# K's inverse norms as rows through DRAM from the third head on, and all of these transfers on SyncE's queue

## The reference, cut to what matters

```python
kv = _rmsnorm(x, kv_norm) @ w_kv
k_sh = _rmsnorm(kv[..., :QK_WIDTH].reshape(b, s, N_HEADS, 2, HEAD_DIM), k_norm)
...
q = (h @ w_q).reshape(b, s, N_HEADS, 2, HEAD_DIM)
q = _rmsnorm(q, q_norm) * (HEAD_DIM ** -0.5)
sc = jnp.einsum('bqhcd,bkhcd->bhcqk', qi, k).astype(jnp.float32)
...
p = jax.nn.softmax(sc, axis=-1)
a = p[:, :, 0] - lam * p[:, :, 1]
...
o = _rmsnorm(o, subln) * (1.0 - lambda_init)
```

## Time and profile before

| what | value |
| --- | --- |
| time, median of 3 runs (lowest, highest) | 941.27 us (940.96, 941.45) |
| the profiled execution, its own time | 941.54 us |
| its span in the profile | 939.7 us |
| PE busy, share of the span | 934.1 us, 99% |
| PEld (weight loads) | 771.6 us, 82% |
| DVE | 683.8 us, 73% |
| ACT | 470.7 us, 50% |
| POOL | 89.8 us, 10% |
| chain that ended last: PE, DVE, ACT, DMA, issue | 91%, 4%, 2%, 2%, 1% |
| DMA queue of SyncE (q1) | 85632 packets, 98.31 MB |
| DMA queue of ScalarE (q10) | 1824 packets, 1.61 MB |

### The profile page before, as it was taken

How to read it: one execution, slowest core, us unless ns; L and a number is a source line. 1 busy time by engine, 2 the same in 40 slices (tenths; PEclk the granted TensorE clock), 3 DMA queues, 4 the chain that set the end, 5 groups by cost and what they waited for, 6 DMA issues and landing times.

```text
span 939.7 us, 11721 instructions
## 1 busy us (share of the span) xinstructions
PE 934.1 (99%) x4439; PEld 771.6 (82%) x4439; DVE 683.8 (73%) x989; ACT 470.7 (50%) x614; POOL 89.8 (10%) x70
## 2 busy tenths in 40 slices
PE   9999999999999999999999999999999999999998
PEld 7888888888888888888888887888888888888887
DVE  6876766676676689988887886757766676667685
ACT  7644343333434438787777773535334333433441
POOL 3000000100000002123222220000100000010010
PEclk9999999999999999999999999999999999999999
DMA  7328682494556644233333232336485458248535
GB/s 258 105 90 239 153 234 90 99 264 129 135 142 173 179 85 120 71 107 93 102 103 103 90 101 90 90 91 188 126 248 155 122 121 250 90 92 225 175 90 135
DMA packets 101583, 130.45 MB, mean 139 GB/s; under 512 B 4297, under 2 KB 63481, under 8 KB 101537
## 3 DMA queue, kind: packets, MB, share of 16 engines
q1 hardware_dynamic: 85632, 98.31, 32.0%
q0 software_dynamic: 14080, 29.91, 17.5%
q10 hardware_dynamic: 1824, 1.61, 0.7%
HBM read 127.69 MB, written 4.75 MB: 141 GB/s over the span
## 4 chain that ended last, share of the span: by engine, by line
PE 91%; DVE 4%; ACT 2%; DMA 2%; issue 1%; SPq 0%; ACTq 0%; DVEq 0%
PE bank L1695 28%; PE bank L1697 28%; PE bank L1696 28%; PE bank L1967 2%; PE bank L1957 1%; DMA raw<-in_w_mlp_out_dram 1%; DVE w_low L1080 1%; PE bank L1996 1%; DMA work<-in_x_dram 1%; PE bank L1872 1%; DVE a_low_buf L1163 0%; ACT w_high L729 0%; ACT w_high L666 0%; PE bank L1938 0%; PE bank L1806 0%
## 5 line engine op out<-in xcount | busy, mean ns | idle before, releaser
L1695 PE MATMUL bank<-h_high_buf,w_high 128*128 128x512 f32 x640 | 252.2, 394 | 0.0
L1697 PE MATMUL bank<-h_high_buf,w_low 128*128 128x512 f32 x640 | 249.5, 390 | 0.0
L1696 PE MATMUL bank<-h_low_buf,w_high 128*128 128x512 f32 x640 | 249.1, 389 | 0.0
L1695 PE MATMUL bank<-w_high,a_high_buf 128*128 128x512 f32 (+1 forms) x452 | 176.1, 390 | 0.1
L1697 PE MATMUL bank<-w_high,a_low_buf 128*128 128x512 f32 (+1 forms) x452 | 175.1, 387 | 0.0
L1696 PE MATMUL bank<-w_low,a_high_buf 128*128 128x512 f32 (+1 forms) x452 | 175.1, 387 | 0.0
L1080 DVE TENSOR_TENSOR w_low<-raw,w_high 128x2048 fp32r<-128x2048 f32 (+2 forms) x56 | 120.3, 2148 | 51.4 <-ACT w_high L729 31.8
L1695 PEld LDWEIGHTS bank<-h_high_buf,w_high 128*128 128x128 f32 x640 | 120.2, 188 | 26.5 <-issue 2.2
L1697 PEld LDWEIGHTS bank<-h_high_buf,w_low 128*128 128x128 f32 x640 | 120.1, 188 | 25.5
L1696 PEld LDWEIGHTS bank<-h_low_buf,w_high 128*128 128x128 f32 x640 | 120.3, 188 | 24.1
L738 ACT ACTIVATE work<-work 128x512 f32<-128x512 f32 x64 | 40.0, 632 | 177.9 <-DVE work L1147 177.9
(11 more groups left out here) (187 smaller groups left out, 1162.5 us busy)
## 6 DMA issues: line engine op xcount, KB each, us to landing
raw<-in_w_mlp_out_dram SPq DMA_DIRECT2D x24, 1024.0 KB, 6.8
raw<-in_w_mlp_out_dram POOLq DMA_DIRECT2D x24, 1024.0 KB, 8.5
raw<-in_w_mlp_in_dram SPq DMA_DIRECT2D x16, 1024.0 KB, 6.2
work<-in_w_mlp_out_dram SPq DMA_DIRECT2D x8, 1024.0 KB, 5.1
work<-in_w_mlp_in_dram SPq DMA_DIRECT2D x8, 1024.0 KB, 7.6
raw<-in_w_kv_dram SPq DMA_DIRECT2D x16, 512.0 KB, 4.0
xT<-in_w_mlp_out_dram SPq DMA_DIRECT2D x8, 1024.0 KB, 4.8
xT<-in_w_mlp_in_dram SPq DMA_DIRECT2D x8, 1024.0 KB, 7.0
```

The source lines that it names most:

```text
L1695: pe.matmul(acc, w_hi, m_hi, start=start, stop=False, skip_group_check=onto)
L1696: pe.matmul(acc, w_hi, m_lo, start=False, stop=False, skip_group_check=onto)
L1697: return pe.matmul(acc, w_lo, m_hi, start=False, stop=stop, skip_group_check=onto)
```

## The change

From the third head on (n = 2 to 7, made in passes 1 to 6), K's inverse norms take the way through DRAM that o's take:

- K's part and Q's part of the statistics are separate: `k_sums`, `k_roots`, `k_inverses`, then `q_sums`, `q_roots`, `q_inverses`. K's come first on VectorE and ScalarE.
- The turn of K's squares moves from behind Q's projection into it, between its fifth and sixth step. The turn back of the spread inverses and the spreading copy are gone.
- The reciprocal writes K's 8 columns grouped by vector; SyncE stores them as two rows of 512 in DRAM (128x2x4 numbers) and loads each row into 64 partitions of `ksq`. VectorE multiplies `kf` by `ksq` read with a step of four (`k_norm_rows`).
- Both transfers of o's row move from ScalarE's queue to SyncE's. The order on SyncE in a pass is: K and Q's weights, K's rows, V's weights, o's row.
- GpSimd's subtraction of K's half of the weights also waits for `k_inverse` of the same pass.

```diff
 # SyncE
+            def spread_k_rows(n):
+
+                sp.wait_ge(k_inverse, n - 1)
+                sp.dma_start(k_row.rearrange("c (p i) -> p c i", p=P), kq_rstd_buf[:, 0:8].rearrange("p (c i) -> p c i", c=2))\
+                  .then_inc(k_row_stored, 16)
+                sp.wait_ge(k_row_stored, 16 * n - 16)
+                sp.wait_ge(kn_ready, n)
+                for c in range(2):
+                    sp.dma_start(ksq[c * HD:(c + 1) * HD, :], k_row[c:c + 1, :].to_broadcast([HD, S])).then_inc(k_row_landed, 16)
...
+            with sp.Fori(4, H) as n:
+                load_kq(n)
+                spread_k_rows(n - 1)
+                load_v(n)
+                spread_o_row(n - 3)
 # GpSimd
+                if h >= 2:
+                    pool.wait_ge(k_inverse, h - 1)
 # ScalarE, head
                     split_high_first(n + 1, kq_landed(n + 1))
+                k_roots(n)
                 square_q(n)
...
-                kq_roots(n)
+                q_roots(n)
...
-                store_o_row(h - 1)
...
-                load_o_row(h - 1)
 # VectorE
+            def k_inverses(n):
+
+                dve.wait_ge(k_rooted, n - 1)
+                dve.reciprocal(kq_rstd_buf[:, 0:8].rearrange("p (c i) -> p i c", c=2), kq_root_buf[:, 0:8].rearrange("p (i c) -> p i c", c=2))\
+                   .then_inc(k_inverse, 1)
...
+            def k_norm_rows(n):
+
+                dve.wait_ge(k_row_landed, 32 * n - 32)
+                k = kf.rearrange("p (i n) -> p i n", i=TT)
+                dve.tensor_tensor(k, k, ksq.rearrange("p (n i) -> p i n", i=TT), ALU.mult).then_inc(kn_ready, 1)
...
                     split_low(U_HEAD + 1 + 2 * n, 0, 1024)
+                    k_sums(n, I[0])
                     o_sums(h - 1, I[3])
-                kq_sums(n, I[0], O[3], first)
-                kq_inverses(n)
+                    k_inverses(n)
+                    q_low(n)
+                    q_sums(n, O[3])
+                    q_inverses(n)
...
-                k_norm(n, I[0])
+                if first:
+                    k_norm(n, I[0])
+                else:
+                    k_norm_rows(n)
 # TensorE
+                    project(None, 1, 1024, I[1], a_high_buf, a_low_buf, None, range(0, 5))
+                    turn_ksq(n, I[0])
+                    project(None, 1, 1024, I[1], a_high_buf, a_low_buf, w_used, range(5, KC))
...
-                turn(ksq, I[0], k_spread, n, k_turned)
```

More of the change, by code:

```diff
@@ L240, in build_program @@
         SUM_BANK = [I[0], I[1], I[2], I[3], O[2], O[3], I[1], I[3]]
+        k_row = nc.dram_tensor("k_rstd_rows", (2, S), F32, kind="Internal").ap()
         o_row = nc.dram_tensor("o_rstd_row", (S,), F32, kind="Internal").ap()
@@ L285, in build_program @@
         w_used = sem("w_used")
+        k_total = sem("k_total")
+        k_rooted = sem("k_rooted")
+        k_inverse = sem("k_inverse")
+        k_row_stored = sem("k_row_stored")
+        k_row_landed = sem("k_row_landed")
         consts_ready = sem("consts_ready")
@@ L531, in _, with load_kq @@
             load_mlp(0)
-            with sp.Fori(0, H) as n:
+            def load_kq(n):
                 slot_free(U_HEAD + 2 * n)
@@ L536, in _, with load_v, spread_o_row @@
                 sp.dma_start(tile3(raw[1][:, 1024:2048], KC), wq_v[:, :, bass.ds(n * P, P)]).then_inc(w_landed[1], 16)
+            def load_v(n):
                 slot_free(U_HEAD + 1 + 2 * n)
                 sp.dma_start(tile3(raw[0][:, 0:1024], KC), wk_v[:, :, bass.ds(D + n * P, P)]).then_inc(w_landed[0], 16)
+            def spread_k_rows(n):
[6 more added lines that the diff above has]
+                    sp.dma_start(ksq[c * HD:(c + 1) * HD, :], k_row[c:c + 1, :].to_broadcast([HD, S])).then_inc(k_row_landed, 16)
+            def spread_o_row(m):
+                sp.wait_ge(o_inverse, m + 1)
+                sp.dma_start(o_row.rearrange("(p i) -> p i", p=P), o_rstd_buf[:, :]).then_inc(o_row_stored, 16)
+                sp.wait_ge(o_row_stored, 16 * m + 16)
+                if not isinstance(m, int) or m > 0:
+                    sp.wait_ge(o_ready, m)
+                sp.dma_start(o_rstd_bc, o_row.rearrange("(a n) -> a n", a=1).to_broadcast([P, S])).then_inc(o_row_landed, 16)
+            with sp.Fori(0, 3) as n:
+                load_kq(n)
+                load_v(n)
+            load_kq(3)
+            spread_k_rows(2)
+            load_v(3)
+            spread_o_row(0)
+            with sp.Fori(4, H) as n:
+                load_kq(n)
+                spread_k_rows(n - 1)
+                load_v(n)
+                spread_o_row(n - 3)
             for f in range(NF):
@@ L549, in _ @@
                           .then_inc(w_landed[u % 2], 16)
+                    if u == U_WO:
+                        spread_k_rows(H - 1)
+                    elif u == U_WO + 1:
+                        spread_o_row(H - 3)
             load_mlp(1)
@@ L1018, in head @@
                 k_high(n)
-                if not second:
-                    act.wait_ge(o_row_landed, 16 * h - 16)
-                store_o_row(h - 1)
                 bias_scale(n, (2, 3))
@@ L1027, in head @@
                 o_squares(h, I[3])
-                if not second:
-                    act.wait_ge(o_ready, h - 1)
-                load_o_row(h - 1)
             first_head()
@@ L2042, in head @@
                     pe.wait_ge(w_low, U_HEAD + 2 + 2 * n)
-                if not first:
-                    turn_ksq(n, I[0])
                 turn_probs(h)
@@ L2048, in head @@
                     pe.wait_ge(w_low, U_HEAD + 2 + 2 * n)
-                project(None, 0, 0, I[2], h_high_buf, h_low_buf, None, range(3, 6) if first else range(0, 5))
-                turn(ksq, I[0], k_spread, n, k_turned)
-                project(None, 0, 0, I[2], h_high_buf, h_low_buf, w_used, range(6 if first else 5, KC))
+                if first:
+                    project(None, 0, 0, I[2], h_high_buf, h_low_buf, None, range(3, 6))
+                    turn(ksq, I[0], k_spread, n, k_turned)
+                    project(None, 0, 0, I[2], h_high_buf, h_low_buf, w_used, range(6, KC))
+                else:
+                    project(None, 0, 0, I[2], h_high_buf, h_low_buf, w_used)
                 if not first:
```

36 lines of the change are left out of this document (26 added, 10 removed).

## The result

The changed kernel takes **950.62 us** (median of 6 runs, 949.39 to 951.36), the kernel before 941.57 on the same chip (940.96 to 942.36): ratio 1.0095, 95% interval 1.0082 to 1.0108. It is slower by some 9 us where the prediction had 942.6, no difference, and at most 945.6. The profiled execution has a span of 949.3 us, 9.6 more than before.

What follows compares the result with a forecast made beforehand. TensorE bounds before (24.34 us a pass); after, the VectorE chain through DRAM does: 7.85 + 6.73 + 9.80 = 24.38 against TensorE's 23.98. With +0.3 at the end and 1.0 for first stores: 942.6 us, range 940.0 to 945.6.

Steps and rivals of the forecast that it cites:

- What costs nothing: Later V weights and o's row, and ScalarE losing two DMA issues but gaining a wait for K's sum: nothing held.
- B to C: VectorE, from K's norm multiply to the head's first combine: 6.73 us against 6.34, the multiply taking 0.39 more.
- C to A: VectorE, from the head's first combine to the next start of V's low-half weights: softmax work, stays 9.80 us.
- A to B: VectorE, from V's low-half weights to K's norm multiply, now through DRAM: 7.85 us against 7.81, bounds 7.4 and 8.6.
- the loads: K's two row loads from DRAM on SyncE's queue: 3.2 us together, the second issued 0.33 later.
- the floor: Q's add, blocked by GpSimd's first subtraction, keeps K's multiply at least 7.7 us behind V's low-half weights, however fast the DMAs.
- The first stores: K's first two stores to DRAM may take 1.4 and 1.0 us extra; 1.0 of the 2.4 was taken.
- TensorE's 2.2 us: Removing the turn back of K's inverses saves net 0.36 us a head over six heads, if TensorE stays the bound.
- The end: The end of the heads moves as pass 6's K norm multiply plus 0.39 does: +0.3 us, before first-store costs.
- (1): Rival: TensorE stays the bound, with K's multiply 7.45 us or less behind V's low-half weights; 939.3 us, chance 0.10.
- (2): Rival: DRAM way between K's inverse and multiply is slower; 945.4 us at d 8.2, deciding from 7.97; chance 0.33.
- (3): Rival: SyncE's queue order makes a weight unit land late, one stall of about 4 us: 945; chance 0.07.

Runs made afterwards that it cites:

- e2: The kernel before with only o's two row transfers moved from ScalarE's to SyncE's queue, nothing of K's changed: 946.59 us, ratio 1.0051.
- e5: e2 with GpSimd's high-half subtraction made to wait for VectorE's bias copies: 941.78 us, ratio 1.0000 to the kernel before.
- e6: The changed kernel with o's two row DMAs back on ScalarE's queue, K's rows staying on SyncE's: 944.10 us, ratio 1.0026 to the kernel before.
- e10: The kernel before with a one-cell memset added on VectorE directly ahead of its last two bias copies: 947.30 us, ratio 1.0059.
- e3: The changed kernel without K's store, loads and the wait for them, so K isn't normalized: 948.73 us, ratio 1.0068 to the kernel before.
- e1: The changed kernel with GpSimd's high-half subtraction made to wait for VectorE's last bias copy: 946.14 us, ratio 1.0047 to the kernel before.
- e7: e1 without K's store, loads and their waits, so K isn't normalized: 943.21 us, ratio 1.0013 to the kernel before.
- e8: e1 with VectorE's wait for GpSimd's subtraction moved from ahead of the first combine to behind the second: 944.35 us, ratio 1.0029 to the kernel before.
- e11: The kernel before without the four transposes turning K's inverses back, nothing in their place, K not normalized: 939.67 us, ratio 0.9975.
- e13: e8 with V's weights issued ahead of K's store and loads on SyncE's queue: 956.39 us, ratio 1.0153 to the kernel before.
- e4: The kernel before with GpSimd's high-half subtraction made to wait for VectorE's bias copies: 941.84 us, ratio 1.0000.
- e9: e8 with K's two rows loaded by a single DMA instead of two: 978.19 us, ratio 1.0383 to the kernel before.
- e15: e8 with V's weights ahead of K's rows on SyncE and VectorE's two first bias copies ahead of K's norm multiply: 956.36 us.
- e16: e15 with o's row on ScalarE's queue and no added wait on GpSimd's high-half subtraction: 956.10 us.

## Why the prediction was wrong, step by step

- **"What costs nothing", ScalarE.** This is the step that failed. "ScalarE loses two DMA issues" was booked as nothing held, and B to C took it that "everything behind it on ScalarE and GpSimd moves by 0.39: 6.73". That assumes that VectorE's second copy stays ahead of GpSimd's start; it was ahead by 0.02 us. The lost issue moved GpSimd ahead by 0.04, and the one that comes second waits until the other is done (2.2 us for the copy, 0.3 for GpSimd). e2 (one edit, +4.9), e5 (the 4.9 gone), e6 (-6.5) and e10 (+5.7 from one cell) show it. The hint stood in the earlier trace rows: a subtraction of 2.69 where the same instruction takes 2.39 in pass 6 is one that had come second, and only just.
- **B to C, 6.73.** Right where no copy is held: 6.74 in pass 3, 6.72 to 6.77 in e6. Held, 7.88 to 7.90: three passes x 1.15 = 3.45 of the 8.75.
- **C to A, 9.80.** 9.80 and 9.81 in two passes, 10.39 and 10.08 where the clock was 0.50; with the late K turn behind it (A to B 8.96 and 8.95, where the passes ahead of them have 8.05 and 8.42), the two falls go with 0.8 and 1.5 us, 2.3 of the 8.75. The prediction had no clock term. No run changes the clock alone, but e3 has a held copy in pass 2 with the clock at 1.00 and in pass 4 with a fall:

```profile
444.41:469.66 25.25, 23.74 (x133) 19.40 (x131) 21.70 (x56) 18.54 (x42) 5.84 (x4) 1.00 0.35 96
...
494.25:520.16 25.91, 24.24 (x127) 19.62 (x126) 21.88 (x56) 18.51 (x42) 5.82 (x4) 0.93 0.36 94
```

  C to A is 9.79 in the first and 10.47 in the second, and A to B of the pass behind 8.06 and 8.96: 1.6 us more with the fall. e2, whose copies are held at an idle time of 0.92 and a clock of 1.00, loses only 1.1 to 1.3 a pass.
- **A to B, 7.85.** 8.05 and 8.42 in passes 2 and 4 of the changed kernel, which follow no fall of the clock, 8.02 in the mean of e1's passes 2 to 5. The term that was too small is the loads: 3.7 and 4.1 there, not 3.2, of which the second issue, 0.55 instead of 0.33, explains less than half. What makes up the rest stays open. Over five passes the 8.02 make 0.9 us, the 8.05 and 8.42 1.9. The store was right in passes 2 to 5 (1.57), and the last one, 2.41, was 0.8 too short in the sum; the floor was nearly right (7.57). The first stores, put at 1.0, cost nothing here: the first took 1.56, and A to B of pass 1 is 9.03 without any store, too (e7). In other runs the first did take 3.0 (e6, e8), with 9.32 and 9.46 from A to B, so that term is real there, at 0.3 to 0.4; the second was 1.57 each time. The 7.81 that the prediction compared with is also the shortest of the kernel before; passes 3 to 5, which wait for TensorE, have 8.16 to 8.22.
- **TensorE's 2.2 us.** The removal gives 2.25 (e11), but with K's turn left in its old place, so the nearness to 2.2 is in part luck: the sum's net of 0.36 a head stays unmeasured. In the changed kernel it was lost to a chain longer than TensorE's, as said.
- **The end.** Right: B of pass 6 comes 9.24 later (557.62 against 548.38), and the end of the span 0.36 more, with 0.39 predicted.
- **The rivals.** (1) had no part. (2) was half right: d, 8.02 to 8.42, lies beyond its turning point of 7.97, and what is left without the held copies is +2.5 (e6, whose first pass has a clock of 0.93). But most of the loss came from elsewhere. (3), a late weight unit, didn't occur, and no weight copy waits for a DMA in the changed kernel; but the queue's order does matter by 12 us the other way round (e13), which the prediction didn't see.

Together: 950.62 less 941.57 is 9.05, of which 6.5 go when o's DMAs return to ScalarE, and 2.5 are left. For these the candidates are K's multiply (0.39 a pass), the DRAM way (2.9 between e1 and e7) and GpSimd's later start, less what TensorE gains; no run splits them in e6.

## What to carry to other kernels

- Where two engines compete for one resource that is given whole, read who comes first and by how much before costing any edit at nothing, even one that only removes work from a third engine. An instruction that takes 10% longer in some passes than in others is the sign (2.69 against 2.39 here).
- If such a race is close, fix its order by a wait (e1, e5) instead of leaving it to hundredths of a microsecond. Where TensorE was the bound the wait was free (e4, e5); where it was not, it made B to C 0.3 longer (e1).
- A small store that someone waits for goes ahead of the bulk loads on its queue, and a broadcast load keeps a wide slowest dimension.

## What the runs showed of the hardware

- VectorE's copy of 128x512 takes 0.48 us (e10, pass 6), and 2.66 if GpSimd's subtraction comes first (e10, passes 2 to 5); the other way round GpSimd loses only 0.3. A hundredth or two decides: with GpSimd's start 0.33 or 0.34 behind the first copy's either of them was first (e6, e10).
- With a DMA issue of 0.33 us that begins 0.14 into its high half of K, ScalarE's next instruction comes 0.02 to 0.03 later (before, passes 2 to 5, against e2). In passes 1 and 6 the issue begins 0.01 before and 0.06 into it, and there is no delay (0.53 and 0.54 against 0.52 and 0.54).
- A DMA of 256 KB with a slowest dimension of 2 takes some 8.5 us from issue to use on two engines (e9; 49 GB/s in the window shown); the same bytes in two DMAs of 64 partitions, 3.7.
- A 4 KB store takes 1.57 us in passes 2 to 5 and 3.2 to 4.5 behind 512 KB on its queue (e13). The first was 1.6 in three kernels and 3.0 or more in the others.
- TensorE's granted clock fell to 0.50 after each of three idle times of 1.65 us (passes 2 and 4 here, pass 4 of e3), but not after one of 1.76 (pass 1 of e15). After 1.46 to 1.48 it fell three times (pass 5 of e3, pass 4 of e13, pass 3 of e16) and twice didn't (pass 5 here, pass 2 of e3). After 0.92 to 0.98 it never did (e2 and e10, four times each). In pass 1 of e6 it fell behind two idle times of 0.63 and 0.77, in pass 1 of e8 it didn't behind 0.78 and 0.77. The length of one idle time doesn't settle it.
